# Extra TensorE products in three waits between the output projection and the first expert tile

## The chip, the cores and the metric

The kernel runs on one core of one Trainium2 chip. A core has a matrix engine (TensorE, PE in the profile), VectorE (DVE), ScalarE (ACT), GpSimd (POOL) and SyncE (SP), each with its own instruction stream; they meet through semaphores. Data lies in SBUF, products are written to PSUM (8 banks of 512 float32 columns by 128 partitions), and 16 DMA engines move data between main memory (HBM) and SBUF. The metric is the device time of one execution in microseconds, smaller is better. Before the change it is 1016.02 us, the median of 3 runs.

## The reference

One decoder layer on 1024 tokens of width 1024, float32: adaLN modulation, a sparse and a differential attention, an output projection with residual, and a mixture of 32 experts in 4 groups. What matters here is the end of the attention part and the routing:

```python
x = x + gate_a[:, None] * jnp.dot(o, w_out[l])
h = rms_norm(x, g_moe[l]) * (1.0 + scale_m[:, None]) + shift_m[:, None]
# hier_moe(h): top-1 group, then top-2 experts inside that group
g_sel = jnp.argmax(g_logits, axis=-1)
top_v, top_i = lax.top_k(e_logits, EXPERT_TOPK)          # 8 logits of the chosen group
for e in range(N_EXPERTS):
    hid = jax.nn.silu(jnp.dot(h, w_gate[e])) * jnp.dot(h, w_up[e])
    y = y + gates[:, e:e + 1] * jnp.dot(hid, w_down[e])
x = x + gate_m[:, None] * y                                # then rms_norm
```

Each expert has gate and up weights of 1024x256 and down weights of 256x1024, so 3 MB each, about 100 MB in all.

## The kernel before

The kernel is one program with an instruction stream per engine, in an order written out by hand. The change touches only the stream of TensorE, `@block.tensor`, in the part that leads from the output projection to the expert tiles.

**Output projection and routing.** A loop over t (0 to T+1, with T = 8 blocks of 128 tokens) works on several blocks at once. `project_out(n)` (L1891) computes one half, 512 columns, of a block's output projection: 8 products with a 128x128 stationary and 512 moving columns, accumulated in PSUM bank n % 4. L1948 transposes the block before it, L1970 computes its 36 router logits. VectorE picks group and experts from these (`route`, L1312 to L1334), counting with `sel_in` when a block's choices are there and with `runs` when they are added to the tally. `choose(q)` on TensorE (L1904, L1905) then computes for every token how many tokens before it chose each expert, into bank 7. VectorE turns that into places in expert tiles (`place_tokens`, L1379 to L1370: `rank_read` at L1382 once the ranks are read, then one-hots, `oh_done`). TensorE's `list_tokens` (L1912, L1915) multiplies these one-hots by token numbers in bank 2, which gives the list of tokens of every tile; blocks 0 to 5 are listed at t = T, and blocks 6 and 7 at the end.

**The end of this part**, in TensorE's order: at t = T the logits of block 7, `choose(6)`, and the list of blocks 0 to 5; at t = T+1 `choose(7)`, which waits for VectorE's choices of the last block; after the loop the product of the totals (L1981), which waits for `runs` and `rank_read`; the list of blocks 6 and 7, which waits for VectorE's one-hots (`oh_done` 12) and increments `sel_ps`; then a wait for `route_done`. VectorE reads the lists (L1448, L1449) and increments `route_done`. GpSimd then gathers the rows of the first two tiles with indirect DMAs (L706, `xg_in`).

**Expert tiles.** There are NSTEP = 20 tiles of 128 places, and each can hold rows of up to four experts. For a tile TensorE transposes the gathered rows (`turn_rows`, L1993, into banks 0 and 1), computes gate and up (`gate_up`, L2006, bank 2 or 3), transposes the hidden values (L2015) and projects down (L2029, banks 5 and 6). ScalarE and VectorE copy the transposed rows with scale and shift (L966 and L1528) and form silu(gate) * up (L974, L1509, L1511). The weights of the experts lie in a ring of 6 slots. SP issues their loads (L419 for gate and up, L423 for down); the first six experts are loaded during the output projection and the routing, and the seventh and later ones each wait until the tile that last used their slot is through gate/up (`gu_ps`) or down. The two last down loads of the first six and a row of the modulation (L573) are issued once the gathers of the first two tiles have landed.

At the end, products with the identity as stationary (`add_into`, L2067) help to add the residual and the experts' rows.

Of the kernel before, what the change touches and what calls it, by code (L numbers as in the profile page):

```python
# [15 lines left out]
BANK = 512  # L16
# [49 lines left out]
def hybrid_layer(nc, x, c, w_ada, b_ada, g_attn, w_in, g_kv, w_uk, w_uv, lam_q1, lam_k1, lam_q2, lam_k2,  # L66
                 g_sub, w_out, g_moe, w_group, b_group, w_router, b_router, w_gate, w_up, w_down, g_final, out):
    _, S, D = x.shape
    T = S // P
    KC = D // P  # L70
    _, NH, LAT, DH = w_uk.shape
    DV = g_sub.shape[1]
    QD = lam_q1.shape[1]
# [80 lines left out]
    with ctx:  # L154
        def sb(name, shape, dt=F32):
            return ctx.enter_context(nc.sbuf_tensor(name, shape, dt))
# [26 lines left out]
        HT = sb("HT", [P, KC, S])  # L183
# [5 lines left out]
        ident = sb("ident", [P, P])  # L189
# [51 lines left out]
        PS = ctx.enter_context(nc.psum_tensor("PS", [P, 8, BANK], F32))  # L241
# [379 lines left out]
        def _(pool):  # L621
# [64 lines left out]
            for i, t in enumerate(sel_tiles):  # L686
                w = P * (t + 1)
                sc = SC[:, sc_off[t]:sc_off[t] + w]
                above, _, run = (a[:, 0:w] for a in sel_tmp[i % 2])
                pool.wait_ge(sel_kept, i + 1)  # L690
                link(pool.tensor_tensor(run, run, above, ALU.add))
                link(pool.tensor_scalar(run, run, -1.0, -NEG, ALU.add, ALU.mult))
                pool.tensor_tensor(sc, run, dist(t), ALU.add).then_inc(sel_done, 1)
# [898 lines left out]
        def _(pe):  # L1592
# [56 lines left out]
            for j in range(KC):  # L1649
# [11 lines left out]
                for n in range(2):  # L1661
                    end = pe.matmul(PS[:, n, :], WI[:, j, LAT:LAT + P], HT[:, j, BANK * n:BANK * (n + 1)],
                                     start=(j == 0), stop=(j == KC - 1))
# [16 lines left out]
            for t in range(T):  # L1680
# [4 lines left out]
                for j in range(KC):  # L1685
                    end = pe.matmul(PS[:, 4 + t % 2, 0:LAT + IH], HT[:, j, P * t:P * (t + 1)], WD[:, j, :],
                                     start=(j == 0), stop=(j == KC - 1))
# [193 lines left out]
            def project_out(n):  # L1881

                if n >= 4:
                    pe.wait_ge(op_sb, n - 3)
                if n == 2 * EARLY + 4:

                    pe.wait_ge(eid_done, 1)
                for k in range(KC):
                    if n == 2 * EARLY + 3 and k == KC // 2:
                        send_places()  # L1890
                    end = pe.matmul(PS[:, n % 4, :], HT[:, k, P * (n // 2):P * (n // 2 + 1)],  # L1891
                                     wo[:, k, BANK * (n % 2):BANK * (n % 2 + 1)], start=(k == 0), stop=(k == KC - 1))
                end.then_inc(op_ps, 1)

            pe.wait_ge(wo_in, 16)
            def choose(q):

                pe.wait_ge(sel_in, q + 1)
                if q >= EARLY:
                    pe.wait_ge(rank_read, (q - EARLY) // 2 + 1)  # L1900
                at = PS[:, 7, NE * q:NE * (q + 1)]
                if q:
                    pe.wait_ge(runs, q)
                    pe.matmul(at, ones[:, :], tally[:, q - 1, :], start=True, stop=False)  # L1904
                pe.matmul(at, earlier[:, :], chosen[:, q, :], start=(q == 0), stop=True).then_inc(rank_ps, 1)  # L1905

            def list_tokens(bank, q0, q1, tiles, rows, low, high, first=True, last=True):

                for q in range(q0, q1):
                    for k in range(2):  # L1910
                        at = PS[:, bank, 0:2 * tiles]
                        pe.matmul(at.rearrange("p (a n) -> p a n", a=2), rows[:, k, q, :],  # L1912
                                  low[:, k, q, :].unsqueeze(1).to_broadcast([P, 2, tiles]),
                                  start=(first and q == q0 and k == 0), stop=False)
                        end = pe.matmul(at, rows[:, k, q, :], high[:, k, q, :], start=False,  # L1915
                                         stop=(last and q == q1 - 1 and k == 1))
                return end

            def send_places():
# [8 lines left out]
                                     ident[0:NE, 0:NE], start=True, stop=True)  # L1928
                end.then_inc(sel_ps, 1)

            for t in range(T + 2):
                if t < T:
                    project_out(2 * t)
                if t == 0:
                    pe.wait_ge(cols_sb, 2)
                    pe.wait_ge(wgr_in, 32)
                    for j in range(KC):
                        end = pe.matmul(PS[:, 7, 0:NR], mcol[:, j:j + 1].to_broadcast([P, P]), wgr[:, j, :],
                                         start=(j == 0), stop=(j == KC - 1))
                    end.then_inc(cols_ps, 1)  # L1940
                if 1 <= t <= T:
                    q = t - 1
                    pe.wait_ge(x2_half, 2 * q + 2)
                    for h in range(2):
                        if q:
                            pe.wait_ge(h2T_sb, 2 * (q - 1) + h + 1)
                        for i in range(4):
                            end = pe.transpose(PS[:, 4 + h, P * i:P * (i + 1)],  # L1948
                                                XT[:, q, P * (4 * h + i):P * (4 * h + i + 1)], ident[:, :])
                        end.then_inc(h2T_ps, 1)  # L1950
                if 2 <= t < T:
                    if t != EARLY + 2:
                        choose(t - 2)
                    if t == EARLY + 1:
                        pe.wait_ge(runs, EARLY)
                        pe.wait_ge(lg_sb, EARLY)
                        pe.matmul(PS[0:NE, 6, 2 * NE:3 * NE], ones[:, 0:NE], tally[:, EARLY - 1, :], start=True, stop=True
                                  ).then_inc(sel_ps, 1)
                if t < T:
                    project_out(2 * t + 1)  # L1960
                if t == EARLY + 2:
                    choose(t - 2)
                if 1 <= t <= T:
                    pe.wait_ge(h2T_sb, 2 * q + 2)
                    if q == 0:
                        pe.wait_ge(wgr_ready, 2)
                    else:
                        pe.wait_ge(lg_sb, q)
                    for j in range(KC):
                        end = pe.matmul(PS[:, 6, 0:NR], h2T[:, q % 2, P * j:P * (j + 1)],  # L1970
                                         wgr[:, j, :], start=(j == 0), stop=(j == KC - 1))
                    end.then_inc(lg_ps, 1)
                if t >= T:
                    choose(t - 2)
                if t == T:
                    pe.wait_ge(op_sb, 2 * T)
                    pe.wait_ge(oh_done, 8)
                    list_tokens(2, 0, EARLY + 2, NSTEP, row_is, low_tok, high_tok, last=False)
            pe.wait_ge(runs, T)
            pe.wait_ge(rank_read, 3)  # L1980
            pe.matmul(PS[:, 7, T * NE:(T + 1) * NE], ones[:, :], tally[:, T - 1, :], start=True, stop=True).then_inc(rank_ps, 1)  # L1981
            pe.wait_ge(oh_done, 12)
            list_tokens(2, EARLY + 2, T, NSTEP, row_is, low_tok, high_tok, first=False).then_inc(sel_ps, 1)
            pe.wait_ge(route_done, 1)


# [64 lines left out]
            with pe.If(n_ov > 0):  # L2051
                pe.wait_ge(ov_rows, 4)
                list_tokens(3, 0, T, NOV, ov_row_is, ov_low, ov_high).then_inc(sel_ps, 1)
                with pe.Fori(0, NOV // 2) as i:
                    for b in range(2):
                        with pe.If(n_ov > 2 * i + b):
                            n = 2 * i + (NSTEP + b)
# [46 lines left out]
```

## Time and profile before

| | us |
|---|---|
| median of 3 runs (1015.51 to 1017.2) | 1016.02 |
| profiled execution, its own time | 1018.29 |
| its span, from first to last instruction | 1016.4 |
| PE busy | 946.8 (93%) |
| DVE busy | 593.9 (58%) |
| ACT busy | 401.1 (39%) |
| POOL busy | 117.9 (12%) |

The profile is of one execution. A matmul in float32 stands in it as two records, so 8 products are "x16". The records overlap, since products are pipelined; the cost of a product in a row of them is the distance between starts. PEclk is the clock that TensorE was granted, as a share of 2.4 GHz. The idle time of an engine stands in brackets with what ended it.

### The profile page before, as it was taken

To read this page: it belongs to the slowest core of one execution; us is meant where nothing else is said; L and a number is where in the kernel's file an instruction comes from. 1 tells how busy PE (TensorE), PEld (TensorE's weight loads), DVE (VectorE), ACT (ScalarE), POOL (GpSimd) and SP (SyncE) were. 2 spreads that over 40 slices of the span, in tenths; PEclk is the share of its full clock that TensorE was granted. 3 is DMA by queue.
4 is the path that set the end of the run, shared out by engine and by line. 5 is a ranking of instruction groups with operands and counts; after the bars stand their busy time and mean duration, and the time that the engine had idled before them with its cause. 6 is when DMAs were issued, how large, how long until landed. Compare 5 with 4: busy or idle time off the path is not lost.

```text
span 1016.4 us, 14951 instructions
## 1 busy us (share of the span) xinstructions
PE 946.8 (93%) x5302; PEld 514.1 (51%) x5302; DVE 593.9 (58%) x1593; ACT 401.1 (39%) x909; POOL 117.9 (12%) x218
## 2 busy tenths in 40 slices
PE   3899999999999999999999999996699999979975
PEld 3464575444448756777766455554233433323421
DVE  2388647999999699987777234366222333212217
ACT  6131235666650488777668121212111221111113
POOL 3001000000008411110000000000111111111003
PEclk9999999999999899999999999998799999989988
DMA  9997100110111000040000421198799999999979
GB/s 325 331 358 266 42 22 23 41 42 23 41 42 27 1 1 2 1 182 9 1 2 1 186 83 63 66 368 325 278 404 421 420 420 420 419 422 420 394 291 373
DMA packets 70956, 191.96 MB, mean 189 GB/s; under 512 B 10264, under 2 KB 37200, under 8 KB 58592
## 3 DMA queue, kind: packets, MB, share of 16 engines
q1 hardware_dynamic: 62896, 173.15, 44.7%
q0 software_dynamic: 5760, 16.78, 4.2%
q10 hardware_dynamic: 2224, 1.05, 0.4%
q8 instruction: 43, 0.70, 0.3%
q14 instruction: 33, 0.27, 0.1%
HBM read 173.12 MB, written 22.04 MB: 192 GB/s over the span
## 4 chain that ended last, share of the span: by engine, by line
PE 65%; DVE 21%; DMA 6%; issue 5%; ACT 1%; POOL 1%; SPq 0%; POOLq 0%; DVEq 0%; ACTq 0%
PE PS L2006 12%; PE PS L1891 11%; DVE BIAS L1157 8%; PE PS L1784 6%; PE PS L2029 5%; PE PS L1827 5%; PE PS L1849 4%; DMA SC<-in_w_up_dram 3%; PE PS L1745 3%; PE PS L1697 3%; PE PS L1844 2%; DMA X<-residual_rows 2%; DVE X L1221 2%; PE PS L1993 2%; PE PS L1722 2%
## 5 line engine op out<-in xcount | busy, mean ns | idle before, releaser
L1697 PE MATMUL PS<-HT,X 128*128 128x512 f32 x384 | 168.8, 593 | 0.0
L2006 PE MATMUL PS<-QKV,HT 128*32 128x512 f32 (+2 forms) x640 | 131.2, 611 | 3.3 <-ACT HT L966 1.7
L870 ACT ACTIVATE X<-X,nmx 128x128 f32<-128x128 f32 (+7 forms) x128 | 98.4, 770 | 54.4 <-DVE nmx L1221 54.1
L1697 PEld LDWEIGHTS PS<-HT,X 128*128 128x128 f32 x384 | 72.5, 190 | 92.4 <-issue 92.4
L1891 PE MATMUL PS<-QKV,HT 128*128 128x512 f32 x256 | 113.7, 597 | 0.0
L1509 DVE TENSOR_TENSOR HT<-PS,HT 128x256 f32<-128x256 f32 x20 | 8.5, 424 | 153.7 <-ACT HT L974 153.7
L1157 DVE TENSOR_SCALAR_CACHE_REDUCE BIAS<-SC,tk 128x384 f32<-128x384 f32 (+3 forms) x128 | 96.4, 809 | 1.1
L853 ACT ACTIVATE X<-SC,tk 128x896 f32<-128x896 f32 x64 | 69.6, 1088 | 43.0 <-DVE tk L1145 43.0
L1784 PE MATMUL PS<-QKV 64*128 64x512 f32 (+3 forms) x384 | 81.3, 530 | 1.6 <-DVE nmx L1221 1.1
L1891 PEld LDWEIGHTS PS<-QKV,HT 128*128 128x128 f32 x256 | 47.4, 190 | 53.7 <-issue 53.6
L2029 PE MATMUL PS<-QKV,HT 128*32 128x512 f32 (+2 forms) x320 | 65.4, 595 | 1.8 <-DMA X<-in_w_down_dram 1.8
L1827 PE MATMUL PS<-ident,X 128*128 128x128 f32 x432 | 64.0, 281 | 1.9 <-DVE X L1239 1.9
L974 ACT ACTIVATE HT<-PS 128x256 f32<-128x256 f32 x20 | 7.7, 384 | 143.8 <-PE PS L2006 143.8
L2006 PE MATMUL PS<-SC,HT 128*32 128x512 f32 (+2 forms) x144 | 58.2, 607 | 6.0 <-issue 6.0
L2006 PEld LDWEIGHTS PS<-QKV,HT 128*32 128x32 f32 (+2 forms) x640 | 38.2, 121 | 49.3 <-issue 46.5
L1221 DVE CUSTOM_DVE_ANT_0 X<-PS,R 128x128 f32<-128x128 f32 (+7 forms) x80 | 50.8, 674 | 17.8 <-PE PS L1784 11.8
L2006 PE MATMUL PS<-X,HT 128*32 128x512 f32 (+2 forms) x160 | 58.8, 626 | 0.8 <-DVE HT L1528 0.8
L1827 PEld LDWEIGHTS PS<-ident,X 128*128 128x128 f32 x432 | 48.1, 142 | 10.5 <-issue 8.6
L1221 DVE CUSTOM_DVE_ANT_0 X<-PS,SC 128x1024 f32<-128x1024 f32 (+5 forms) x48 | 42.0, 887 | 17.9 <-PE PS L1784 17.8
L1784 PEld LDWEIGHTS PS<-QKV 64*128 64x128 f32 x384 | 32.4, 190 | 28.6 <-issue 20.7
L1519 DVE TENSOR_TENSOR HT<-PS,R 128x512 f32<-128x512 f32 x40 | 27.7, 692 | 30.1 <-PE PS L2029 26.9
L1844 PEld LDWEIGHTS PS<-QKV,HT 128*128 128x128 f32 x288 | 35.6, 196 | 18.1 <-ACT HT L891 9.2
(296 smaller groups left out, 1489.3 us busy)
## 6 DMA issues: line engine op xcount, KB each, us to landing
QKV<-in_w_gate_dram SPq DMA_DIRECT2D x22, 1024.0 KB
QKV<-in_w_up_dram SPq DMA_DIRECT2D x22, 1024.0 KB
QKV<-in_w_down_dram SPq DMA_DIRECT2D x22, 1024.0 KB
QKV<-in_w_ada_dram SPq DMA_DIRECT2D x8, 2048.0 KB, 13.5
QKV<-in_w_ada_dram SPq DMA_DIRECT2D x8, 1024.0 KB, 12.5
X<-in_w_in_dram SPq DMA_DIRECT2D x16, 512.0 KB, 3.8
QKV<-expert_rows SPq DMA_DIRECT2D x16, 512.0 KB, 10.7
X<-in_w_gate_dram SPq DMA_DIRECT2D x5, 1024.0 KB
```

What stands on the lines that cost most here:

```text
L853: act.activation(RL[:, n % 2, 0:w], SC[:, sc_off[t]:sc_off[t] + w], ACT.Sign, bias=tk[:, 4, i:i + 1].bitcast(F32), scale=-1.0, accum_out=c ...
L870: act.activation(sc, sc, ACT.Exp, bias=nmx[:, i % 4, m:m + 1], scale=-1.0, accum_out=rs[:, i, m:m + 1]).then_inc(exp_done, 1)
L1157: dve.tensor_scalar(BIAS[:, i % 3, 0:w], SC[:, sc_off[t]:sc_off[t] + w], thr.bitcast(F32)[:, i:i + 1], 0.0, ALU.is_lt, ALU.add, accum_out= ...
L1221: dve.tensor_tensor_reduce(sc_buf[i % 4][:, m, 0:w], PS[:, 2 * m:2 * m + 2, :].rearrange("p a n -> p (a n)")[:, BANK * n:BANK * n + w], aw ...
L1697: end = pe.matmul(PS[:, 2 * b + half, :], WS[:, b, j, :], HT[:, j, BANK * half:BANK * (half + 1)], start=(j == 0), stop=(j == KC - 1))
L1784: end = pe.matmul(PS[:, 2 * m + n + c0 // BANK, 0:c1 - c0], QKV[rows_m, q0:q0 + P], QKV[rows_m, k0 + c0:k0 + c1], start=True, stop=True)
L1827: end = pe.transpose(PS[:, 4 + g % 2, c0:c0 + P], sc_buf[i % 4][:, m, P * b:P * (b + 1)], ident[:, :])
L1844: end = pe.matmul(PS[:, 6 + h % 2, slot], turned_at(i)[:, g % 4, P * (b - b0):P * (b - b0 + 1)], vf[:, u * S + P * b:u * S + P * (b + 1)], ...
L1849: end = pe.matmul(PS[DH * m:DH * (m + 1), 6 + h % 2, slot], vd[:, b, v0:v0 + DH], turned_at(i)[:, g % 4, c0:c0 + P], start=(b == 0), stop= ...
L1891: end = pe.matmul(PS[:, n % 4, :], HT[:, k, P * (n // 2):P * (n // 2 + 1)], wo[:, k, BANK * (n % 2):BANK * (n % 2 + 1)], start=(k == 0), s ...
L2006: end = pe.matmul(PS[at, 2 + b, :], hgT[b][:, P * c_ + at.start:P * c_ + at.stop], WGU[w][:, c_, :, :], start=(c_ == 0), stop=(c_ == KC - 1))
L2029: end = pe.matmul(PS[at, 5 + h, :], hidT[b][:, P * c_ + at.start:P * c_ + at.stop], WDN[w][:, c_, BANK * h:BANK * (h + 1)], start=(c_ == 0 ...
```

## The change

A function `keep_warm(n)` is added to TensorE's stream. It issues n products of the identity matrix (128x128) with the upper 512 columns of the last eighth of the tile HT, into PSUM bank 3, each with start and stop set. Nobody reads these results, and the function neither waits for a semaphore nor increments one. It is called at three places: 5 products behind the list of blocks 0 to 5 at t = T, 7 behind the product of the totals, and 14 behind the list of blocks 6 and 7. At these places bank 3 has been read by VectorE (`op_sb` is at 2T), and the next to write it is the gate/up group of the second tile.

```diff
+            def keep_warm(n):
+
+                for _ in range(n):
+                    pe.matmul(PS[:, 3, :], ident[:, :], HT[:, KC - 1, BANK:2 * BANK], start=True, stop=True)
+
             for t in range(T + 2):
...
                 if t == T:
                     pe.wait_ge(op_sb, 2 * T)
                     pe.wait_ge(oh_done, 8)
                     list_tokens(2, 0, EARLY + 2, NSTEP, row_is, low_tok, high_tok, last=False)
+                    keep_warm(5)
             pe.wait_ge(runs, T)
             pe.wait_ge(rank_read, 3)
             pe.matmul(PS[:, 7, T * NE:(T + 1) * NE], ones[:, :], tally[:, T - 1, :], start=True, stop=True).then_inc(rank_ps, 1)
+            keep_warm(7)
             pe.wait_ge(oh_done, 12)
             list_tokens(2, EARLY + 2, T, NSTEP, row_is, low_tok, high_tok, first=False).then_inc(sel_ps, 1)
+            keep_warm(14)
             pe.wait_ge(route_done, 1)
```

Nothing else is changed.

## Rows read from the trace of the kernel before

**Rows 1.** Page, part 2: granted clock and DMA rate in 40 slices of 25.4 us.

```profile
PEclk9999999999999899999999999998799999989988
GB/s 325 331 358 266 42 22 23 41 42 23 41 42 27 1 1 2 1 182 9 1 2 1 186 83 63 66 368 325 278 404 421 420 420 420 419 422 420 394 291 373
```

**Rows 2.** Chain of waits, in order of time: start us, us, what.

```profile
711.20 5.68 DMA HT<-h_rows,lst
...
720.62 9.53 PE PS L2006 x64
...
732.90 7.07 PE PS L2006 x64
739.97 1.09 PE PS L1993 x8
```

**Rows 3.** Timeline of PE, 698 to 721: start, us, engine, line, [idle before <-releaser].

```profile
698.87 1.98 PE L1970 MATMUL PS<-wgr,SC 128*128 128x36 f32 x16 [1.05 <-ACT SC L949]
...
702.05 0.20 PE L1915 MATMUL PS<-R,BIAS 128*128 128x40 bf16 x1
704.88 0.64 PE L1904 MATMUL PS<-BIAS,ones 128*128 128x32 f32 x2 [2.63 <-DVE BIAS L1330]
...
706.54 0.60 PE L1981 MATMUL PS<-BIAS,ones 128*128 128x32 f32 x2 [0.59 <-DVEq L1382]
709.63 0.21 PE L1912 MATMUL PS<-R,BIAS 128*128 128x40 bf16 x1 [2.48 <-DVE BIAS L1370]
...
717.02 1.94 PE L1993 MATMUL PS<-ident,HT 128*128 128x128 f32 x8 [6.95 <-DMA HT<-h_rows,lst]
720.62 1.07 PE L2006 MATMUL PS<-QKV,HT 128*32 128x512 f32 x2 [1.66 <-ACT HT L966]
```

**Rows 4.** Stretches: us, busy PE PEld DVE ACT POOL, PEclk, DMA share, GB/s.

```profile
702.00:704.00 2.00, 0.25 (x8) 0.13 (x4) 1.72 (x9) 0.00 (x0) 0.00 (x0) 0.50 0.98 381
...
725.00:726.00 1.00, 1.00 (x12) 0.20 (x8) 0.00 (x0) 0.00 (x0) 0.00 (x0) 0.75 1.05 426
726.00:727.00 1.00, 1.00 (x16) 0.33 (x12) 0.00 (x0) 0.00 (x0) 0.00 (x0) 1.00 0.96 401
...
729.00:730.00 1.00, 1.00 (x12) 0.12 (x4) 0.00 (x0) 0.00 (x0) 0.00 (x0) 1.00 0.01 0
...
888.00:892.00 4.00, 2.34 (x23) 0.83 (x14) 1.38 (x2) 0.38 (x1) 0.71 (x1) 1.00 1.00 414
```

**Rows 5.** Timeline of PE in the output projection.

```profile
644.95 7.11 PE L1891 MATMUL PS<-QKV,HT 128*128 128x512 f32 x16
651.90 1.04 PE L1948 MATMUL PS<-ident,X 128*128 128x128 f32 x8
...
653.23 0.25 PE L1957 MATMUL PS<-BIAS,ones 128*32 128x32 f32 x2
```

**Rows 6.** Timeline of PE near the end, the products with the identity as stationary.

```profile
980.13 9.49 PE L2067 MATMUL PS<-X,ident 128*128 128x512 f32 x16 [5.89 <-DMA X<-residual_rows]
989.46 7.03 PE L2067 MATMUL PS<-QKV 128*128 128x512 f32 x16
```

**Rows 7.** Timeline of DVE, 705 to 711.

```profile
705.98 0.22 DVE L1379 TENSOR_TENSOR BIAS<-PS,cact 128x64 f32<-128x64 f32 x1 [0.93 <-PE PS L1905]
...
710.11 0.18 DVE L1448 TENSOR_SCALAR lst<-PS 128x20 int32<-128x20 f32 x1 [0.54 <-PE PS L1915]
```

**Rows 8.** Timeline of SP, 717 to 731: the DMAs that it issues.

```profile
717.57 0.33 SPq L573 DMA_DIRECT2D R<-modulation_row  x1
...
730.87 0.34 SPq L419 DMA_DIRECT2D QKV<-in_w_gate_dram  x1
```

**Rows 9.** Timeline of PE, 886 to 912: the rows with idle time before them.

```profile
886.10 0.63 PE L2029 MATMUL PS<-QKV,HT 128*32 128x512 f32 x3 [1.83 <-DMA X<-in_w_down_dram]
891.83 0.61 PE L2006 MATMUL PS<-QKV,HT 128*64 128x512 f32 x1 [1.66 <-DMA SC<-in_w_up_dram]
909.70 1.03 PE L2006 MATMUL PS<-SC,HT 128*32 128x512 f32 x1 [5.68 <-issue]
```

## The prediction

> **What bounds the kernel now.** I read the profile's page first, for the granted clock of TensorE and the DMA rate in 40 slices [rows 1]: the clock is at its upper level nearly everywhere, with a dip in slices 28 and 29 of 25.4 us each (686 to 737 us), and the DMA engines run at about 420 GB/s from slice 30 on, but at 278 GB/s in slice 28. The change sits in that dip. Then the chain of waits, in order of time, from the last output projection on [rows 2]: it goes DVE (routing of the last block), PE (two small products), DVE (places of the last two blocks), PE (the token lists), DVE, the gather DMA of 5.68 us, PE (transposes), ScalarE, and PE's first gate/up group of 9.53 us, where the second takes 7.07. So the path alternates between engines, and PE's idle times are waits for a link of the same path. The timeline of PE [rows 3] gives the idle times: 2.63 us up to 704.88, 0.59 up to 706.54, 2.48 up to 709.63, 6.95 up to 717.02, and 1.66 up to 720.62. The three that the change fills are the first, the third and the fourth, 12.06 us together. The stretches [rows 4] show the granted clock at 0.50 (1.2 GHz) from 702 on, back to 1.00 (2.4 GHz) only in the course of 725 to 726, about 4.9 us after the first gate/up group began.
>
> **What one added product costs.** The change adds 5 + 7 + 14 = 26 products with a 128x128 stationary and 512 moving columns, all float32. No instruction of that line exists before, but the same shape does. One half of an output projection is 8 such products: they stand as x16 records (two per product), start at 644.95, and the next group starts at 651.90 [rows 5], so 6.95/8 = 0.87 us each at the full clock. Near the kernel's end stand 8 products with the identity in float32, exactly the operands' kinds of the change: they begin after a 5.89 us idle time and take 9.49 us, and the 8 ordinary ones behind them 7.03 [rows 6]. The difference of 2.46 us is a cold stretch of 4.9 us at half speed, as long as in the first gate/up group. So a product of the identity costs no less than another, and such products do bring the clock back: at half clock all through, eight would have taken 14.
> One rule speaks for a much cheaper product. The Trainium skill (TensorE: Matmul & The Clock Gate, section Back-to-back issue gap) has successive products start N ÷ 2.4 GHz + 2.5 ns apart, measured for bf16, which is 0.216 us for 512 columns; by it the 26 would take 5.6 us and fit the waits. The rows above have the same columns in float32 at four times that, so the sum goes by 0.87.
> 26 x 0.87 = 22.6 us of products stand against 12.06 us of waits. PE takes its work in program order and the products wait for nothing, so what doesn't fit delays the instruction behind.
>
> **The sum, step by step** (against the profiled execution; its span is 1016.4, its own time 1018.29, that is 1.89 around the span, and 2.27 above the median of 1016.02; I carry the difference over to the median).
> 1. Five products. PE is free at about 702.1 (last list product starts at 702.05 [rows 3]). At full clock they take 4.35 us, against a wait of 2.63. The clock is low there, and how soon it rises is not in the trace: the ends are at once (0) and 4.9 us, which add 0 or 2.4 us. I take the middle, +1.2: the products end at 707.6, and the two products that rank the last block start there and not at 704.88. DVE resumed 1.10 us after their start at half clock (704.88 to 705.98 [rows 3, 7]); at full clock about 0.6. It resumes at 708.2, 2.2 late.
> 2. Seven products. The totals' product (706.54) starts 0.56 us after DVE resumes, so at 708.8, and takes 0.2 like its warm like at 653.23 [rows 5]. The seven run from 709.0 for 6.1 us, to 715.1. DVE's one-hots, done at 709.6 before, are done at 711.8, so the token lists now wait 3.3 us for products that nobody reads. DVE reads the lists 0.45 us later, at 715.5, not 710.11 [rows 7]: 5.4 late.
> 3. Fourteen products. The gather starts at 711.2 + 5.4 = 716.6 and, at no more than its 5.68 us [rows 2], lands by 722.3. The fourteen run from 715.3 for 12.2 us, to 727.5. The first transposes therefore start at 727.5 and not 717.02: 10.5 late, and the gather isn't what they wait for any more. Whether it becomes faster on quieter queues costs or gives nothing.
> 4. What the warm clock gives back. Eight transposes take 1.09 (at 739.97) instead of 1.94 [rows 2, 3]: -0.85. The step of ScalarE up to the gate/up group is unchanged. The gate/up group takes 7.0 instead of 9.53 [rows 2]: -2.5.
> Sum at the end of the first gate/up group: 10.5 - 0.85 - 2.5 = +7.1 us.
> 5. From there to the end. The next weights are issued by SP at 730.87 [rows 8], 0.7 us after this group ends, into the slots that it frees, and between 729 and 730 the DMA engines move nothing [rows 4]. So the weight stream starts again with this group, late by the same 7.1, and PE behind it too, whichever of the two is the bound later. The modulation row that SP issues once the gathers have landed (717.57 [rows 8]) and two down weights behind it go out some 5 us later and have the 15 us up to the end of gate/up to hide in; without that cover 2 MB would cost 5 us at 420 GB/s [rows 1].
> The three calls add no wait and no semaphore; product and reader share bank 3 only with projections already read. I take contention at nothing: DVE reads the banks 6, 7 and 2, not 3. Bounds of the sum: +5.9 with the clock up at once in step 1, +8.3 with it up after 4.9 us, and 2.45 more if it falls once in the 1.66 us before gate/up, so +10.8. In 888 to 892 there are waits of 1.83 and 1.66 us close together [rows 9], and the clock stays at 1.00 [rows 4]; that is why I leave this fall out of the sum.
>
> **Rivals.**
> A. The products fit and the change pays. If a product cost one record's pitch, 0.43 us, the three calls would take 2.2, 3.0 and 6.0 us, against 2.63, 2.48 and 6.95. The counts suit that price strikingly. Then the ranking would be done 0.5 sooner, the lists 0.4 sooner in all, and with 0.85 and 2.5 from the clock the first group ends 3.75 sooner: 1012.3 us. Against it: two records for each product in every row of that shape. Decided by the price of a product, with the border near 0.64 us (16.6 us, that is 702.1 to 717.02 less 1.7 of PE's own work between, plus the 3.35 given back, over 26). The price of the page cited above would give the same, as everything fits.
> B. The overrun is absorbed. Later PE waits for weights: 1.83, 1.66 and 5.68 us (886 to 910) [rows 9], 9.17 in all, more than 7.1. If the weight stream didn't depend on the first group, being late there would only shorten these waits: 1016.0. Against it: the refill at 730.87 and the empty engines before it.
> C. The clock falls again in the gap before gate/up, or stays low longer in the first call: +10.8, 1026.8 us. For it: a 1.05 us wait with small products behind it [rows 3] was enough for the clock to be down at 702 [rows 4].
>
> **How the numbers follow.** Forecast 0.76, C 0.10, B 0.08, A 0.06. Time: 1016.02 + 7.1 = 1023.1. The forecast's own range is 1021.9 to 1024.3. The range for 8 in 10 takes in C and reaches halfway to B, since part of the lateness might be absorbed: 1018.5 to 1027.5. A difference under 0.2% (2 us) is not told from none here, the three runs lying between 1015.51 and 1017.2. Slower by more than that: 0.76 + 0.10 = 0.86; within: 0.08; faster: 0.06.
>
> **What would show it.** In PE's timeline of the changed kernel: x10, x14 and x28 records of the new line with a busy time of about 5.6, 6.1 and 12.2 us; ranking starting near 707.6 and the lists near 715; no idle time before the first transposes, although the gather landed about 5 us before; granted clock 1.00 from about 705 on; the first gate/up group in 7.0 us, ending near 737. On SP the first refill about 7 us later than 730.87, and the late waits for weights as long as before. I'm wrong if the x28 group takes 6 us (A), if the first group ends 7 us late but the waits near 890 to 910 shrink (B), or if the gate/up group still takes over 8.5 us (C).

## The result and the profile after

The changed kernel takes 1026.3 us (median of 6 runs, 1024.23 to 1027.58) against 1016.06 us before (6 runs): ratio 1.0099, 95% interval 1.0085 to 1.0113, so 8.6 to 11.5 us slower. A second set of runs gave 1025.22 against 1017.15 us, ratio 1.0084 (1.0062 to 1.0105). The profiled execution took 1027.1 us with a span of 1025.2 (1018.29 and 1016.4 before).

The page, granted clock and DMA rate [rows 1]: the 28th and 29th digits of the clock, 8 and 7 before, are now 8 and 9. The 29th DMA rate is 202 GB/s and not 278.

```profile
PEclk9999999999999899999999999998999999989988
GB/s 325 326 358 260 42 22 41 22 41 42 21 42 27 1 2 1 32 156 2 2 2 45 175 69 62 167 343 269 202 406 421 420 419 420 419 421 420 394 296 358
```

The timeline of PE in the changed kernel, same columns as [rows 3]. The lines behind the new function have moved: L1975 is the logits, L1934 the added product, L1987 the totals, L2001 the transposes, L2014 gate/up.

```profile
696.62 3.63 PE L1975 MATMUL PS<-wgr,SC 128*128 128x36 f32 x16 [1.05 <-ACT SC L949]
700.06 0.61 PE L1904 MATMUL PS<-BIAS,ones 128*128 128x32 f32 x2
...
701.73 7.04 PE L1934 MATMUL PS<-HT,ident 128*128 128x512 f32 x10
708.61 0.30 PE L1904 MATMUL PS<-BIAS,ones 128*128 128x32 f32 x2
...
709.74 0.38 PE L1987 MATMUL PS<-BIAS,ones 128*128 128x32 f32 x2 [0.60 <-DVEq L1382]
709.95 6.25 PE L1934 MATMUL PS<-HT,ident 128*128 128x512 f32 x14
...
716.25 12.26 PE L1934 MATMUL PS<-HT,ident 128*128 128x512 f32 x28
728.35 1.05 PE L2001 MATMUL PS<-ident,HT 128*128 128x128 f32 x8
731.05 0.62 PE L2014 MATMUL PS<-QKV,HT 128*32 128x512 f32 x2 [1.65 <-ACT HT L966]
...
738.06 1.16 PE L2001 MATMUL PS<-ident,HT 128*128 128x128 f32 x8
```

The idle times of 2.63, 2.48 and 6.95 us are gone, and what stands in them is longer: 6.9, 6.1 and 12.1 us from start to the next instruction's start. The transposes and the gate/up group are at full clock: 1.05 us, and 7.0 us (731.05 to 738.06) where it was 9.53 [rows 2].

Now the waiting is on the readers' side. The timeline of DVE: it waits 4.80 us for the ranks and 3.67 us for the lists, which it waited 0.93 and 0.54 for before [rows 7].

```profile
709.18 0.22 DVE L1379 TENSOR_TENSOR BIAS<-PS,cact 128x64 f32<-128x64 f32 x1 [4.80 <-PE PS L1905]
...
712.08 0.68 DVE L1370 TENSOR_TENSOR BIAS<-gkv,R 128x512 bf16<-128x512 f32 x1
716.44 0.18 DVE L1448 TENSOR_SCALAR lst<-PS 128x20 int32<-128x20 f32 x1 [3.67 <-PE PS L1915]
```

Stretches, columns as in [rows 4]. The clock (the number behind POOL) is still 0.50 in 704 to 706 and rises in the course of 706 to 708, while the five products run. Between 714 and 716 and between 736 and 738 the DMA engines move nothing, as before between 729 and 730 [rows 4].

```profile
704.00:706.00 2.00, 2.00 (x3) 0.67 (x2) 0.34 (x2) 0.00 (x0) 0.00 (x0) 0.50 0.72 213
706.00:708.00 2.00, 2.00 (x5) 0.91 (x4) 0.00 (x0) 0.00 (x0) 0.00 (x0) 0.80 0.80 274
...
714.00:716.00 2.00, 2.00 (x6) 0.76 (x5) 0.00 (x0) 0.00 (x0) 0.00 (x0) 1.00 0.00 0
...
736.00:738.00 2.00, 2.00 (x20) 0.39 (x12) 0.00 (x0) 0.00 (x0) 0.00 (x0) 1.00 0.00 0
```

SP issues the modulation row at 724.40, once the gathers have landed (they were issued from 717.53 on), and the first refill at 738.90, 8.0 us later than before [rows 8]:

```profile
724.40 0.33 SPq L573 DMA_DIRECT2D R<-modulation_row  x1
...
738.90 0.34 SPq L419 DMA_DIRECT2D QKV<-in_w_gate_dram  x1
```

And the late waits of PE for weights are as long as before, 1.84 and 5.63 us, and 8 us later [rows 9]; the one of 1.66 doesn't stand by itself any more; the chain of waits gives the L2037 group at 894.14 a length of 5.34 us, where others of its kind have 3.57.

```profile
894.14 0.75 PE L2037 MATMUL PS<-QKV,HT 128*32 128x512 f32 x3 [1.84 <-DMA X<-in_w_down_dram]
917.69 1.03 PE L2014 MATMUL PS<-SC,HT 128*32 128x512 f32 x1 [5.63 <-issue]
```

**A measure that leaves out the chance ahead of the change.** The logits of the last block begin at 698.87 before and 696.62 after, and anywhere from 693.6 to 698.9 in the 13 traces of this study, ahead of all that is changed. So I compare the stage from there to the transposes behind the first gate/up group (730.02 before, 738.06 after): 31.15 us and 41.44 us, 10.3 us more. Behind the stage the spans still hold 286.4 and 287.1 us. The row of before:

```profile
730.02 1.16 PE L1993 MATMUL PS<-ident,HT 128*128 128x128 f32 x8
```

### The profile page after: what moved, and what is told of

The parts are those of the page before. It is cut to its first block, busy times and chain, and to the rows that moved or that the text cites. A ratio compares the mean times of both kernels' runs of the same rounds, so it can differ in the third digit from the quotient of the medians.

```text
span 1025.2 us, 15055 instructions
## 1 busy us (share of the span) xinstructions
PE 969.0 (95%) x5354; PEld 523.4 (51%) x5354; DVE 594.0 (58%) x1593; ACT 400.6 (39%) x909; POOL 117.8 (11%) x218
## 3 DMA queue, kind: packets, MB, share of 16 engines
q10 hardware_dynamic: 2224, 1.05, 0.4%
## 4 chain that ended last, share of the span: by engine, by line
PE 67%; DVE 19%; DMA 5%; issue 5%; ACT 1%; POOL 1%; SPq 1%; POOLq 0%; DVEq 0%; ACTq 0%
PE PS L2014 12%; PE PS L1891 11%; DVE BIAS L1157 8%; PE PS L1784 6%; PE PS L2037 6%; PE PS L1827 5%; PE PS L1849 4%; DMA X<-in_w_down_dram 3%; PE PS L1745 3%; PE PS L1697 3%; PE PS L1934 2%; PE PS L1844 2%; DVE X L1221 2%; PE PS L1722 2%; PE PS L2001 2%
## 5 line engine op out<-in xcount | busy, mean ns | idle before, releaser
L2014 PE MATMUL PS<-QKV,HT 128*32 128x512 f32 (+2 forms) x640 | 129.1, 604 | 1.7 <-ACT HT L966 1.7
L2037 PE MATMUL PS<-QKV,HT 128*32 128x512 f32 (+2 forms) x320 | 67.1, 613 | 1.8 <-DMA X<-in_w_down_dram 1.8
L2014 PE MATMUL PS<-SC,HT 128*32 128x512 f32 (+2 forms) x144 | 58.5, 609 | 5.6 <-issue 5.6
L2014 PEld LDWEIGHTS PS<-QKV,HT 128*32 128x32 f32 (+2 forms) x640 | 37.9, 119 | 45.3 <-issue 42.6
L2014 PE MATMUL PS<-X,HT 128*32 128x512 f32 (+2 forms) x160 | 56.4, 594 | 0.8 <-DVE HT L1528 0.8
## 6 DMA issues: line engine op xcount, KB each, us to landing
QKV<-expert_rows SPq DMA_DIRECT2D x16, 512.0 KB, 10.3
```

Of the source, the lines that this page charges most:

```text
L2014: end = pe.matmul(PS[at, 2 + b, :], hgT[b][:, P * c_ + at.start:P * c_ + at.stop], WGU[w][:, c_, :, :], start=(c_ == 0), stop=(c_ == KC - 1))
L2037: end = pe.matmul(PS[at, 5 + h, :], hidT[b][:, P * c_ + at.start:P * c_ + at.stop], WDN[w][:, c_, BANK * h:BANK * (h + 1)], start=(c_ == 0 ...
```

## The experiments

All are the changed kernel with other counts, or another kind of product, in the three calls. Nothing of the layer's computation is changed in any of them. A difference to before, such as "+4.6 us", is (ratio - 1) x 1016 us, with the runs of before that were taken beside it; the ratio is an estimate of its own and lies up to 0.0013 from the quotient of the two medians. The stage is read from one trace each, and that execution need not be a typical one: in after_again and bf16_same it was the fastest of its runs, in bf16_fill and before_again the slowest.

| run (counts) | stage, us | median, us | before | ratio (95%) |
|---|---|---|---|---|
| before, 1st trace | 31.15 | 1016.06 | | |
| before_again | 32.34 | 1016.15 | 1015.92 | 0.9999 (0.9981 to 1.0017) |
| changed (5, 7, 14) | 41.44 | 1026.30 | 1016.06 | 1.0099 (1.0085 to 1.0113) |
| after_again (5, 7, 14) | 38.61 | 1025.22 | 1017.15 | 1.0084 (1.0062 to 1.0105) |
| third_only (0, 0, 14) | 35.11 | 1020.19 | 1015.92 | 1.0045 (1.0030 to 1.0059) |
| no_third (5, 7, 0) | 36.32 | 1021.79 | 1015.92 | 1.0052 (1.0034 to 1.0070) |
| first_only (5, 0, 0) | 33.36 | 1018.04 | 1016.25 | 1.0013 (0.9996 to 1.0030) |
| second_only (0, 7, 0) | 36.24 | 1021.34 | 1016.25 | 1.0046 (1.0029 to 1.0063) |
| c_2_2_14 | 34.02 | 1018.29 | 1016.25 | 1.0025 (1.0008 to 1.0042) |
| fitted_2_2_7 | 29.84 | 1014.05 | 1017.15 | 0.9978 (0.9964 to 0.9992) |
| tail_5 (0, 0, 5) | 28.37 | 1014.60 | 1017.15 | 0.9975 (0.9963 to 0.9987) |
| bf16_same (5, 7, 14) | 30.05 | 1014.41 | 1015.92 | 0.9998 (0.9982 to 1.0014) |
| bf16_fill (10, 10, 30) | 28.72 | 1014.86 | 1017.15 | 0.9978 (0.9965 to 0.9991) |

**The kernel before, again.** No edit.

> The kernel before, unchanged, for a second profile. In the changed kernel's trace the clock was down already in the last block's logits (3.63 us for x16 records instead of 1.98), ahead of any added product. If that is chance of the moment (theory), the second trace of before shows the fall at another time than the first (near 701.6), and its span differs by 1 to 2 us. If the change causes it (rival), it is again near 701.6.

Its time is that of before, and the spans of the two traces differ by 0.6 us, not by the 1 to 2 expected. In its trace the last logits take 2.72 us, and the granted clock falls about 699 and not in 701 to 702:

```profile
697.97 2.72 PE L1970 MATMUL PS<-wgr,SC 128*128 128x36 f32 x16 [1.05 <-ACT SC L949]
```

So the early fall in the changed kernel's trace (3.63 us of logits) needs no product that comes after it: the moment of the fall moves from run to run in the unchanged kernel too. In second_only, where nothing is added ahead of the ranking either, the last logits take 3.55 us. The stage of before_again is 32.34 us, 1.2 longer than the first, from the clock alone.

**The changed kernel, again.** No edit.

> The changed kernel once more, for a second profile and a better median. The forecast of +7.1 us had its first call, at half clock for 2.4 us, between +5.9 and +8.3. Theory: the clock is down when the 5 products start and rises 2.4 to 5 us later, according to the moment, so the call takes 5.6 to 7 us and the stage from the last block's logits to the end of the first gate/up group takes 39 to 41.5 us (31.2 and 32.3 in the two traces of before): +8 to +10 us in the median. Rival (something else costs 2 to 3 us behind the first group): the stage takes under 39.5 us, and the rest of the kernel, 286 to 287 us in all traces so far, is longer by 2 us or more.

+8.5 us by the ratio, within the theory's range; the stage, 38.61 us, lies a little under its lower end of 39. The rival that the stage is short and 2 us or more are lost behind it falls, since 287.4 us stand behind it, 1.0 more than in the first trace of before and 0.7 more than in before_again. This trace is of the fastest of the six runs (1021.61 us). Here the clock was still up during the logits, and the five products took 6.2 us:

```profile
693.69 1.97 PE L1975 MATMUL PS<-wgr,SC 128*128 128x36 f32 x16 [1.05 <-ACT SC L949]
...
696.79 6.23 PE L1934 MATMUL PS<-HT,ident 128*128 128x512 f32 x10
```

**Only the third call.**

```diff
-                    keep_warm(5)
-            keep_warm(7)
+                    keep_warm(0)
+            keep_warm(0)
```

> The calls with 5 and 7 products are gone, the one with 14 stays. Theory (products that outlast a wait delay the path, the overruns add up): lists and gather are on time as before; the 14 begin at about 710.1 of the kernel before's time, cold for up to 4.9 us, so 12.2 + 2.4 = 14.6 us, against a wait of 6.95: first transposes 7.7 us late, less 0.85 and 2.5 us from the warm clock: +4.3 us on before, near 1020.4. Rival (the price of the change lies in the first two calls, the third about pays for itself): within 1 us of before. Rival (a product costs half of what I say): 14 fit in the wait, 3 us faster than before.

+4.6 us (3.0 to 6.0), and the stage is 3.4 longer than the mean of the two of before: the theory. The x28 group begins at half clock, lasts 14.4 us (14.6 worked out), and the transposes follow it with no wait, at full clock:

```profile
708.36 14.54 PE L1934 MATMUL PS<-HT,ident 128*128 128x512 f32 x28
722.73 1.04 PE L2001 MATMUL PS<-ident,HT 128*128 128x128 f32 x8
```

**Without the third call.**

```diff
-            keep_warm(14)
+            keep_warm(0)
```

> The call with 14 products is gone, those with 5 and 7 stay. Theory: the lists come as late as in the changed kernel (8.6 us late against the routing in its trace), the gather takes the same 6 us behind them, in this wait TensorE's clock falls again, and transposes and gate/up are cold as before: +6 to +8.6 us on before, near 1023. The third call is then worth only some 2 us of the change's 10. Rival (the third call with its 12 us is the main part): +3 us or less.

+5.3 us (3.5 to 7.1), a little under the theory's 6 to 8.6. In its trace the first call took 5.8 us and not 7, and the gather that the transposes wait for took 4.58 us from issue to landing, where it took 5.68 before [rows 2]. The rest of the mechanism is as expected: the wait for the gather is back, with 5.84 us where it was 6.95, the clock falls in it, and the transposes take 1.95 us again.

```profile
702.32 5.76 PE L1934 MATMUL PS<-HT,ident 128*128 128x512 f32 x10
...
709.26 6.25 PE L1934 MATMUL PS<-HT,ident 128*128 128x512 f32 x14
...
721.55 1.95 PE L2001 MATMUL PS<-ident,HT 128*128 128x128 f32 x8 [5.84 <-DMA HT<-h_rows,lst]
```

From its chain of waits, and from its stretches (columns as in [rows 4]), the gather and the DMA rate when it is issued:

```profile
716.84 4.58 DMA HT<-h_rows,lst
```

```profile
716.00:718.00 2.00, 0.00 (x0) 0.00 (x0) 1.65 (x11) 0.33 (x2) 1.16 (x1) 1.00 0.00 0
```

**The first call alone, the second alone.** Two kernels, each with the other two counts at 0.

> Only the first call, 5 products. Theory: they outlast the wait by 3 to 4.5 us (5.8 to 7 us in the traces so far, against 2.1 to 2.6), the ranking behind them runs at full clock (-0.5), and the clock falls again in the waits behind, so nothing is given back at the gate/up group: +2.5 to +4 on before. Rival (clock held up through later short waits): +1 or less.

> Only the second call, 7 products. Theory: they begin at half clock, 6.1 + 1.2 to 2.4 us = 7.3 to 8.5, against a wait of 2.48, and the lists come 4.8 to 6 us late; in the gather's wait the clock falls again: +4.5 to +6 on before. With first_only the sum is more than the 5.3 of both together, since in the run with both the first call had brought the clock up for the second. Rival (the calls just add): second_only = run with both less first_only, some 2 us.

The first alone costs 1.3 us by the ratio (-0.4 to 3.0), less than the 2.5 expected at the least and not clear of nothing; its stage is 1.6 longer than the mean of the two of before. Its trace shows where the expected lateness went. The lists of blocks 6 and 7 begin 14.6 us after the start of the last logits, against 10.8 and 11.4 in the two traces of before, so the overrun is there, 3.5 us. But the gather behind them took 4.60 us and not 5.7, which gives 1.1 back, and the way from the first transposes to the second took 12.45 us, against 13.0 and 13.5. That the gather would be shorter was not in the theory. The second alone costs 4.7 (2.9 to 6.4), as expected. Their sum, 6.0, is above the 5.3 of both together, but by less than either is uncertain, so that this part of the theory stays open in the times. The traces show its mechanism: the seven products take 8.3 us when they begin at half clock, against 6.25 behind the first call. First the rows of first_only (the last is from its chain of waits), then those of second_only.

```profile
699.54 6.29 PE L1934 MATMUL PS<-HT,ident 128*128 128x512 f32 x10
...
716.19 1.94 PE L2001 MATMUL PS<-ident,HT 128*128 128x128 f32 x8 [5.86 <-DMA HT<-h_rows,lst]
```

```profile
711.45 4.60 DMA HT<-h_rows,lst
```

```profile
706.66 8.33 PE L1934 MATMUL PS<-HT,ident 128*128 128x512 f32 x14
...
721.18 1.95 PE L2001 MATMUL PS<-ident,HT 128*128 128x128 f32 x8 [6.00 <-DMA HT<-h_rows,lst]
```

**Counts that fit the waits.**

```diff
-                    keep_warm(5)
-            keep_warm(7)
-            keep_warm(14)
+                    keep_warm(2)
+            keep_warm(2)
+            keep_warm(7)
```

> The three calls cut to 2, 2 and 7 products. Theory (only what outlasts a wait costs, and a clock that is up gives back up to 3.35 us): the first two take 1.7 each at full clock and 3.5 at half, against waits of 2.1 to 2.6, the last 6.1 to 7.3 against 6.95. Between 1 and 3.4 us faster than before. Rival (any float32 product in these waits costs, as it holds up the next instruction): no faster than before.

2.2 us faster than before (0.8 to 3.7). The first two calls take 3.55 and 3.26 us to the next instruction's start, close to the 3.5 worked out for half clock, and outlast the waits (2.1 to 2.7 and 2.5 us in the traces that leave them empty) by about 1 us each. The transposes follow the seventh product at once and at full clock:

```profile
707.67 6.25 PE L1934 MATMUL PS<-HT,ident 128*128 128x512 f32 x14
713.76 1.04 PE L2001 MATMUL PS<-ident,HT 128*128 128x128 f32 x8
```

**Seven more in the third call.** As above, with 14 in place of 7.

> 2, 2 and 14 products: the run with 2, 2 and 7, and seven more in the third call. There the transposes followed the seventh product at once, at full clock. Theory: every further product is late work at 0.87 us, so 6.1 us slower than with 2, 2 and 7, near +4 on before, and 6.1 us longer in the stage (29.8 to 35.9). Rival (the slack behind the gather takes some of it, or the weight stream absorbs it): under 4 us slower than with 2, 2 and 7.

+2.5 us on before, where near +4 was expected. From ratio 0.9978 to 1.0025 is 4.8 us (the two were set against different runs of before, so some 2 us either way), and the stages differ by 4.2. Both are under the expected 6.1, and the times alone don't exclude the rival's "under 4". For the stage the trace shows why: up to the third call it was 1.8 us shorter by the clock's chance (706.58 - 694.37 against 707.67 - 693.62). From the third call to the transposes it is 12.1 us against 6.1, the 6.0 us that seven products cost.

```profile
706.58 12.26 PE L1934 MATMUL PS<-HT,ident 128*128 128x512 f32 x28
718.68 1.04 PE L2001 MATMUL PS<-ident,HT 128*128 128x128 f32 x8
```

**Five products in the gather's wait alone.**

```diff
-                    keep_warm(5)
-            keep_warm(7)
-            keep_warm(14)
+                    keep_warm(0)
+            keep_warm(0)
+            keep_warm(5)
```

> Only the third call stays, with 5 products instead of 14. Theory: started cold they take up to 4.35 + 2.4 = 6.8 us and end just within the wait of 6.95; where the clock is up by then, transposes and first gate/up group are 3.35 us shorter: 2 to 3.4 us faster than before, and some 7 faster than with 14. Rival (too few products to bring the clock back by then): same as before.

2.5 us faster than before (1.3 to 3.8), and the shortest stage of all, 28.37 us. From fitted_2_2_7 (2.2 us faster) it is not told apart. The products end 0.28 us before the gather lands:

```profile
707.82 7.26 PE L1934 MATMUL PS<-HT,ident 128*128 128x512 f32 x10
715.36 1.13 PE L2001 MATMUL PS<-ident,HT 128*128 128x128 f32 x8 [0.28 <-DMA HT<-h_rows,lst]
718.14 0.62 PE L2014 MATMUL PS<-QKV,HT 128*32 128x512 f32 x2 [1.66 <-ACT HT L966]
```

**The same counts in bfloat16.**

```diff
-                    pe.matmul(PS[:, 3, :], ident[:, :], HT[:, KC - 1, BANK:2 * BANK], start=True, stop=True)
+                    half = ident[:, :].bitcast(BF16)
+                    pe.matmul(PS[:, 3, :].rearrange("p (a n) -> p a n", a=2), half[:, 0:P],
+                              half.unsqueeze(1).to_broadcast([P, 2, 2 * P]), start=True, stop=True)
```

> The same 26 products with 128x128 stationary and 512 moving columns, but in bfloat16 (bits of the identity), in the same places. Theory: what hurts is the fourfold streaming time of float32. At about 0.22 us each at full clock they take 1.1 (up to 2.2 cold), 1.5 and 3.0 us and fit in the three waits, nothing is late: no slower than before. Whether they keep the clock up is open: the first two waits are filled by half or more, the last (6.95 us) by less than half, so the clock may fall before the transposes: between -3.7 and 0 us on before. Rival (the delay comes from something else that the products do, such as memory ports or the PSUM bank): still several us slower than before.

Ratio 0.9998 (0.9982 to 1.0014): no slower than before with the same 26 products of 512 columns into the same bank. So the 10 us are not the price of the instructions or of the bank. The moving operand is another one as well, the identity in place of HT; but fitted_2_2_7 and tail_5 read HT in float32 and are not slower than before, so what is left is the time for which the products occupy PE. One record stands for a product now, and line numbers are two higher than in the changed kernel:

```profile
697.71 2.30 PE L1935 MATMUL PS<-ident 128*128 128x512 bf16 x5
700.18 0.64 PE L1904 MATMUL PS<-BIAS,ones 128*128 128x32 f32 x2 [0.17 <-DVE BIAS L1330]
...
705.46 3.18 PE L1935 MATMUL PS<-ident 128*128 128x512 bf16 x14
711.54 1.54 PE L2003 MATMUL PS<-ident,HT 128*128 128x128 f32 x8 [2.90 <-DMA HT<-h_rows,lst]
```

The seven in the second wait take 3.0 us, at half clock, and outlast it by 0.5. Of the gather's wait 2.90 us are left, and the clock falls during these transposes, so that little is given back at the gate/up group (9.1 us).

**bfloat16, counts that fill the waits.** As above, with 10, 10 and 30.

> bfloat16 products as in the run before, now 10, 10 and 30 of them: 2.2, 2.2 and 6.5 us at full clock, up to 4.3 for the first ones at half. Theory: the waits are filled and hardly outlasted, the clock stays up through transposes and gate/up: lateness of 0 to 2 us in the first two calls, 3.35 us given back: 1 to 3.4 us faster than before. Rival (bfloat16 products do not hold the clock as float32 ones do, since 14 of them had left it to fall): the clock falls in spite of them, no gain.

2.2 us faster than before (0.9 to 3.6). Thirty take 6.47 us up to the next instruction (709.60 to 716.07), 0.216 us each. The rival that bfloat16 products don't hold the clock is out.

```profile
709.60 6.64 PE L1935 MATMUL PS<-ident 128*128 128x512 bf16 x30
716.07 1.05 PE L2003 MATMUL PS<-ident,HT 128*128 128x128 f32 x8
```

Its stage is 3.0 us shorter than the mean of before, but behind the stage come 289.3 us, 2.9 more than in the first trace of before; there the wait for the residual rows near the end is 8.53 us and not 5.89 [rows 6]. With 2, 2 and 7 it is 288.0, with tail_5 286.2. This trace is of the slowest of its twelve runs (1016.98 us against a median of 1014.86). In it, a part of what the stage gains is lost in that wait:

```profile
978.50 9.80 PE L2077 MATMUL PS<-X,ident 128*128 128x512 f32 x16 [8.53 <-DMA X<-residual_rows]
```

The 0.216 us are the warm gap that the Trainium skill (TensorE: Matmul & The Clock Gate, section Back-to-back issue gap) gives for a product of 512 columns, N ÷ 2.4 GHz + 2.5 ns. The same section calls that the gap of an isolated product and gives about 131 ns for a sustained stream; the thirty in a row here don't show that, they stay at 0.216 us. The float32 products of this kernel take four times it, which decides this change.

## Why the prediction was right

The direction, the mechanism and the later steps held; the time of 1023.1 was 3.2 us low in the first set of runs and, by the difference of the medians (8.1 us), 1.0 low in the second. The measured 1026.3 lies within the range of 1018.5 to 1027.5, but outside the forecast's own 1021.9 to 1024.3: it is inside only because the range made room for rival C. C's time of 1026.8 came close by luck, as the fall of the clock that it prices did not happen.

**Price of a product.** 0.87 us worked out; 12.1 us for 14 (0.864) and 6.1 for 7 measured. Rival A, half that price, is out. Its reasoning that cheap products would fit and cost nothing is borne out by the bf16 runs, at a quarter of the price: they are as fast as before or faster.

**Step 1, the term that was mis-sized.** The five products were put at 5.55 us, with the clock low for 2.4 us. They took 6.9 in the first trace, and 6.1, 5.6 and 6.1 in after_again, no_third and first_only, starts to starts. Five at 0.864 are 4.3 us, so the clock was low for twice the rest: 5.1, 3.5, 2.6 and 3.6 us. The middle between "at once" and "4.9 us" was too kind: in every trace a part of the five ran at half clock, and the first lies beyond the upper end. In the first trace there is a second part, which is no cost of the change: the clock had fallen ahead of it, so the last logits (3.63 for 1.98 us) and the ranking of the block before were slow, and the first product began 5.11 us behind the start of the logits and not 3.21. These two, 1.3 and 1.9 us, are the 3.2 us between the forecast of 7.1 and the 10.3 of the stage. The unchanged kernel pays such a fall as well (before_again, +1.2 in the stage), so it belongs to the scatter, not to the sum.

**Step 2.** Seven products 6.1, as predicted; the one-hots are done at 712.76 and the lists begin at 716.04, 3.3 us later, as predicted. **Step 3.** Fourteen 12.1 (12.2), and the transposes wait for no gather. The prediction said that a faster gather would give nothing; that is so here, where the first one lands in 4.6 us and the products still end 6 us behind it, but not in first_only and no_third, which wait for it. **Step 4.** 1.05 and 7.0 us, as predicted. **Step 5.** The refill is 8.0 us later, the late waits are as long as ever, and the span behind the stage is 287.1 for 286.4: rival B is out. Rival C is half right: the clock stayed low longer in the first call, but in no trace with a filled wait did it fall in the 1.65 us before gate/up.

**A misreading.** The slice of 25.4 us with 278 GB/s and a clock digit of 7 is the 29th, 711.5 to 737 us; the 28th has 325 [rows 1]. Nothing in the sum rests on it.

**What each call is worth.** In the order of the code, by the ratios: 1.3 us for the first (not clear of nothing), 5.3 with the second, and 10.1 or 8.5 with the third. The third adds 3 to 5 us to the first two; 12.1 us of products in a wait of 5.84 us, less the 3.4 that the clock gives back, would be 2.9.

**What stays open.** The two sets of the changed kernel differ by 2 us in their difference to before, and the runs of one kernel by up to 6.7 (1012.24 to 1018.90 in before_again). Whether the longer wait for the residual rows in bf16_fill is the rule after an early first tile, or chance, one trace doesn't tell. How much of the scatter is the clock's moment in this stage and how much the 5 us of scatter ahead of it was not separated.

## What to carry to other kernels

Filler work on an in-order engine is free only up to the wait it fills, and that has to be worked out in time, at half clock, for the operands' type: here seven products too many in the last wait turned a gain of 2.2 us into a loss of 2.5. Fill only the wait whose successor is long enough to gain by the clock: five products before the gate/up group gave as much as all three waits filled, and filling the two short waits on the way to it gained nothing that the times can tell. Short bfloat16 products fill a wait in steps of 0.22 us where float32 has 0.87.

## What the runs showed of the hardware

The gather that the transposes wait for was shorter where the weight stream had run dry. From issue to landing it took 5.68 and 5.71 us in the two traces of before and 6.11 in tail_5, with over 410 GB/s moved in the stretch of 2 us in which it is issued and in the next. It took 4.5 to 4.7 us in the other traces but one: in both of the changed kernel, in no_third and in second_only nothing is moved in the stretch of its issue, and in first_only, fitted_2_2_7, c_2_2_14 and the two bf16 runs the rate falls to 31 to 207 GB/s in the next. third_only lies between, with 5.3 us and 414, 434 and 311 GB/s in three stretches. One stretch of before and the same of first_only (columns as in [rows 4]), each right behind a gather's issue (711.20 and 711.45):

```profile
712.00:714.00 2.00, 0.00 (x0) 0.00 (x0) 0.19 (x2) 0.00 (x0) 1.50 (x2) 0.50 0.98 414
```

```profile
712.00:714.00 2.00, 0.00 (x0) 0.00 (x0) 0.41 (x3) 0.00 (x0) 1.69 (x2) 0.50 0.22 31
```

No run changes the weights alone, so the cause is argued from the rates. When both gathers have landed, SP issues its next DMA: that comes 6.4 to 7.2 us after the first gather's issue in all 13 traces, with no such difference.

Products of the identity with itself in bfloat16, most of whose terms are zero, held the clock as those of real data in float32 did: with 30 of them in the gather's wait the transposes took 1.05 us, with 7 or 14 in float32 1.04 or 1.05.
